# A hybrid decoder step on one Trainium2 core: the experts' weight units through six SBUF buffers instead of twelve

## The reference, cut to what matters

```python
def swiglu(x, wg, wu, wd):
    return (jax.nn.silu(x @ wg) * (x @ wu)) @ wd

def moe_swiglu(h, w_r, b_r, wg, wu, wd):
    ...
    top_p, top_e = lax.top_k(probs, TOP_K)              # 2 of 8 experts per token
    ...
    def expert_block(args):
        xblk, e = args
        return swiglu(xblk, wg[e], wu[e], wd[e])
    yb = lax.map(expert_block, (xb, block_e)).reshape(n_slots, dm)
    contrib = yb[dest] * sp[:, None].astype(h.dtype)
    return jax.ops.segment_sum(contrib, stok, num_segments=n_tok)
```

## Time and profile before

| | |
|---|---|
| timed runs, median | 1714.72 us |
| the profiled execution, its own time | 1708.33 us |
| its span, first to last instruction | 1706.5 us |
| TensorE busy | 1607.8 us (94%) |
| VectorE / ScalarE / GpSimd busy | 763.8 / 378.2 / 122.9 us |
| the experts' matmuls, from the first to the last | 790.6 to 1667.9 us |
| DMA moved | 535.7 MB, mean 314 GB/s |

### The profile page before, as it was taken

The page is one execution under the profiler, slowest core; times in us unless marked ns, Lnnn a source line. Parts: engine busy times, 40 slices in busy tenths (PEclk is TensorE's granted clock), DMA queues, the critical chain, the costliest instruction groups (busy, mean ns, idle before and its releaser), DMA issues.

```text
span 1706.5 us, 31161 instructions
## 1 busy us (share of the span) xinstructions
PE 1607.8 (94%) x12948; PEld 902.9 (53%) x12948; DVE 763.8 (45%) x1822; ACT 378.2 (22%) x616; POOL 122.9 (7%) x162
## 2 busy tenths in 40 slices
PE   6996299999999999999999999999999999999993
PEld 3874297899998879864333333333333333333331
DVE  2796155555443998362233422433234233342233
ACT  3444052544424453421001000010010100101012
POOL 0123210100002113011000000000000000000000
PEclk8998599999999999997999999999999999999997
DMA  9889812744455782054899999999999999999995
GB/s 383 348 314 338 290 41 101 300 158 162 173 198 213 282 324 115 7 220 177 325 407 391 420 420 412 420 410 421 420 405 420 412 415 420 407 419 415 413 421 221
DMA packets 82486, 535.73 MB, mean 314 GB/s; under 512 B 9200, under 2 KB 9328, under 8 KB 23600
## 3 DMA queue, kind: packets, MB, share of 16 engines
q1 hardware_dynamic: 70592, 487.46, 71.1%
q0 software_dynamic: 10080, 40.47, 6.5%
q10 hardware_dynamic: 1680, 5.90, 1.0%
HBM read 516.24 MB, written 36.43 MB: 324 GB/s over the span
## 4 chain that ended last, share of the span: by engine, by line
PE 79%; DVE 6%; ACT 1%; DMA 1%; issue 1%; POOL 0%; DVEq 0%; POOLq 0%
PE ps L2386 42%; PE ps L2395 5%; PE ps L2410 4%; PE ps L1871 4%; PE ps L1873 4%; PE ps L1872 4%; PE ps L2060 3%; DVE yc L1315 2%; PE ps L1968 1%; PE ps L1983 1%; PE ps L1981 1%; PE ps L2231 1%; PE ps L2001 1%; PE ps L2368 1%; DVE wlo L1222 1%
## 5 line engine op out<-in xcount | busy, mean ns | idle before, releaser
L2410 PE MATMUL ps<-raw,hT 128*32 128x512 f32 x1008 | 437.2, 592 | 0.0
L2410 PE MATMUL ps<-extra,hT 128*32 128x512 f32 x972 | 421.5, 592 | 0.0
L2386 PE MATMUL ps<-extra,ht 128*32 128x512 f32 x2736 | 403.2, 595 | 0.7 <-DVE ht L1797 0.7
L2386 PE MATMUL ps<-raw,ht 128*32 128x512 f32 x2640 | 387.1, 592 | 0.0
L1809 DVE TENSOR_TENSOR ae<-ps,sge 96x512 f32<-96x512 f32 x56 | 38.5, 687 | 536.7 <-PE ps L2386 536.7
L2386 PEld LDWEIGHTS ps<-extra,ht 128*32 128x32 f32 x2736 | 108.3, 110 | 270.2 <-issue 270.2
L2386 PEld LDWEIGHTS ps<-raw,ht 128*32 128x32 f32 x2640 | 104.1, 110 | 257.8 <-issue 257.8
L1792 DVE STREAM_TRANSPOSE hT<-ae 32x128 f32<-32x128 f32 x672 | 202.8, 302 | 15.7
L1191 ACT ACTIVATE sge<-ps 96x512 f32<-96x512 f32 x56 | 33.2, 593 | 706.9 <-PE ps L2386 706.7
L1871 PE MATMUL ps<-h_hi,whi 128*128 128x288 f32 x560 | 168.2, 300 | 0.2 <-DVE h_lo L1299 0.2
L1872 PE MATMUL ps<-h_lo,whi 128*128 128x288 f32 x560 | 165.9, 296 | 0.0
(11 more groups left out here) (346 smaller groups left out, 1774.4 us busy)
## 6 DMA issues: line engine op xcount, KB each, us to landing
raw<-units SPq DMA_DIRECT2D x279, 1024.0 KB, 11.4
extra<-units SPq DMA_DIRECT2D x174, 1024.0 KB, 13.2
slots_in<-const_in POOLq DMA_DIRECT2D x18, 512.0 KB, 26.3
slots_out<-const_in POOLq DMA_DIRECT2D x18, 512.0 KB, 27.6
raw<-units SPq DMA_DIRECT2D x16, 512.0 KB, 10.9
sst<-gdn_in POOLq DMA_DIRECT2D x8, 512.0 KB, 10.8
gdns_out<-sst POOLq DMA_DIRECT2D x8, 512.0 KB, 4.0
qst_out<-qpad POOLq DMA_DIRECT2D x2, 1890.0 KB, 10.7
```

Of the source, the lines that this page charges most:

```text
L2386: last = mm(ps[rows(t), (0 if kind == "g" else 2) + n % 2, :], ht[n // FC % 2][:, a], weights((kind, n, k // 4), k % 4), start=(k == 0), s ...
L2410: last = mm(ps[GROUPS * GT:P, DOWN_BANK[t][half], :], hidden(n, t, k), weights(("d", n, half), k), start=(c == 0 and first), stop=(n in (F ...
```

## The change

The ring has six buffers, `raw0` to `raw5`. The buffers `extra` and their semaphores are gone, and so is the loading of units in the middle of layer 1. In the loop a load waits for the unit six places ahead of it in `STREAM` instead of twelve. The matmuls, their order and the order of the units stay as they are. At the end six loads more than needed are issued instead of twelve.

```diff
-RING = 2 * NRAW
+RING = NRAW
...
-        extra = [at(f"extra{i}", cursor[0] + i * UNIT * 4, UNIT) for i in range(2 * NSPLIT)]
...
-        extra_in = [sem(f"extra_in{i}") for i in range(2 * NSPLIT)]
...
         def buffer_of(q):
 
-            i = q % RING
-            if i < 2 * NSPLIT:
-                return extra[i], extra_in[i], 16 * (q // RING + 1)
-            r = (U_MOE + i) % NRAW
+            r = (U_MOE + q) % NRAW
             return raw[r], raw_in[r], 16 * (len(range(r, U_MOE, NRAW)) + q // RING + 1)
...
-            split_end = SPLIT_UNITS[-1] + NRAW + 1
             for u in range(U_MOE):
                 load(u)
...
-                if u == split_end:
-                    sp.wait_ge(unit_used, S_MOE)
-                    for q in range(2 * NSPLIT):
-                        load_expert(q)
-            for q in range(2 * NSPLIT, RING):
-                wait_free(U_MOE - NRAW + q - 2 * NSPLIT)
+            for q in range(RING):
+                wait_free(U_MOE - NRAW + q)
                 load_expert(q)
...
-            wait_last(sp, range(2 * NSPLIT))
             sp.wait_ge(y_ready, 1)
             sp.dma_start(y_out[:, 0:KD * T // 2], hf[:, 0:KD * T // 2]).then_inc(y_sent, 16)
-            wait_last(sp, range(2 * NSPLIT + 1, RING))
+            wait_last(sp, range(1, RING))
...
-            _, landed_, value = buffer_of(2 * NSPLIT)
+            _, landed_, value = buffer_of(0)
             pool.wait_ge(landed_, pool.snap(n_pass * PER_BUFFER + value))
```

## The result

The changed kernel takes 1935.63 us (1932.68 and 1938.58), the one before 1714.72 us: a ratio of 1.130, interval 1.125 to 1.135. The forecast was 1846 us and its range ended at 1880. The direction was right, the size was not: 221 us instead of 131.

A forecast was written before the change was run, and what follows sets the result against it. TensorE was taken to set the pace, with the DMA engines nearly full. Stalls 132.3, experts' rows 4 and end -2 made 134 us on 1708.3, so 1842.6; forecast 1846 us, halfway to the timed median's offset, range 1824 to 1880.

The forecast's parts named there:

- What bounds the kernel: Experts' part: TensorE and DMA engines both nearly full; TensorE sets the pace, SyncE's loads wait for buffers still in use.
- The load's lead: Experts' part, slot 8: u0 lands late, TensorE stalls 2.45 us in each of 54 steps, 132.3 us in all.
- The fit of the Trainium skill: Weight loads: 2.0 us fixed plus bytes over 436 GB/s per DMA; stall 1.9 us, 103 us in sum; trace preferred.
- The granted clock: Rival, experts' part: clock falls to half in each stall, 127 us more, 1973 us; chance 0.12.
- The experts' rows: ScalarE's transfers once per expert push u1 0 to 0.9 us late in 7 steps; 4 us taken; what follows fits.
- The end: Kernel's end: fewer unneeded loads ahead of expert 7's last results; between 0 and -4.6 us, -2 taken.
- Slower batches: Rival, experts' part: DMA engines fall to 361 GB/s in short batches, stall 3.3 us, 1892 us; chance 0.07.
- no stall: Rival, experts' part: landing times are all backlog, u0 lands by T + 4.91, 1704 to 1714 us; chance 0.03.
- What would show it right or wrong: Signs in the experts' part: right, some 54 waits of about 2.3 us, clock 1.00; wrong, clock under 1.00, among others.
- the first rival: Experts' part: the granted clock falls in each stall, 127 us more, 1973 us; chance 0.12.
- the first case: Experts' part: one stall of 2.1 to 2.9 us per step, 113 to 157 us; chance 0.78.

The follow-up runs named there:

- lead6: The kernel before with all twelve buffers; only the loop's load waits for the unit six places ahead instead of twelve: 1938.82 us, ratio 1.132.
- fill2: The changed kernel plus two extra matmuls of constants between slot 7 and the wait of slot 8 in steps 2 to 55: 1898.96 us, ratio 1.110.
- rows16: On fill2, 16 instead of 96 rows of `xe` fetched from expert 2 on and of `ye` stored for experts 0 to 6: 1877.46 us.
- after_again: The changed kernel itself, run once more with nothing altered: 1939.24 us, ratio 1.134.
- ring7: The kernel before with a ring of seven buffers, the six raw ones and one extra, instead of twelve: 1803.88 us, ratio 1.052.

## Why the prediction was wrong, point by point

- **What bounds the kernel.** Right: both engines were nearly full, and the load's lead became the limit. lead6 shows it alone.
- **The load's lead, 54 x 2.45 = 132 us.** Right in mechanism, place and size. d0 landed 4.8 and u0 6.8 us after their issues, the step with nothing else in it is 17.95 us (17.90 predicted), and a typical stall is 2.2 us idle plus 0.17 us of restart: 54 x 2.37 = 128 us. The fit of the Trainium skill, page "DMA: Bandwidth & Descriptors", section on the anatomy of one DMA, is given there for DMAs that GpSimd issues, while these loads come from SyncE, which the prediction did not say. Its 4.4 us for one unit would have put the stall at 1.9 us; the trace did not agree.
- **The granted clock.** This is the step that failed: the sum and the range put it at nothing. I gave the fall a chance of 0.12, as a rival, because the clock was still full late in the idle stretch from 156 on the earlier trace rows. The two stretches of 2.2 and 2.5 us that were followed by the lower level were the nearer rows in length, and I set them aside for the sparse matmuls around them. In the changed kernel 16 of the 30 idle stretches of 1.95 to 2.3 us are followed by a fall, 9 of the 13 of 2.3 to 3 us and all 13 longer ones. Nor was it "always or never": the rival priced a fall in every step, 4.7 us long, at 127 us. In fact 38 stretches of 60 had one, 35 of them 3.4 us long and three 6.8, and the trace loses 67 us, of which fill2 got 37 back. A clock that is full during the idle stretch, as in the row from 156 on, also proves little, since most falls come only after the restart. With the clock kept up the time is still 1899 us, above the range's 1880, so the clock is the largest missing term and not the only one. The Trainium skill, "TensorE: Matmul & The Clock Gate", section "Why this matters for your kernels", warned of idle gaps between bursts of matmuls, because the clock can go back to half; the trace agrees, with 38 falls behind 60 stretches that lie between dense matmuls.
- **The experts' rows, 4 us.** The size came out by luck: the waits that follow them make 6.1 us in the changed kernel, but before g0 at slot 0, where I had said that all fits, and not before u1. With the clock kept up, five sixths of the rows cost 21.5 us (rows16).
- **Instruction fetches, not in the sum at all.** 10 stalls with a q8 packet are 1.4 us longer than the typical 2.2 and the seven with a q14 packet about 0.6 us: some 18 us. This is not shown as a cause: it rests on which stalls have a packet in their window, after_again and ring7 bear it out less, and no run took the fetches away.
- **The end, -2 us.** Right in size, by luck: 36.7 us from the last expert matmul to the end of the span, where it was 38.7. The gathering of the rows takes 4.61 us instead of 7.36; the last results still take 7.05, where I had expected the gain.
- **Slower batches, and no stall.** Neither rival came: 2.5 us a unit held in the short batches of the changed kernel, and the landing of a load was not all backlog.
- **What would show it right or wrong** named the clock under 1.00 as the sign of the first rival, and that is what came. The range ended at the first case's dearest value, and so left out the one case for which the trace had two rows.

## What to carry to other kernels

When a ring of buffers is made shorter, count for each load the time from its release to its first use, and set it against the time that one, two and three loads take to an empty queue; the number of buffers alone says little (the order of loading was worth 77 us at the same six). A regular wait of some two microseconds on TensorE can have a second price in the granted clock: look in the trace for idle stretches of that length and at the clock behind them too, and give their fall the weight that those rows have. And when two losses overlap, removing one yields less than its own sum, so measure it before promising it.

## What the runs showed of the hardware that was not expected

- TensorE with 1.7 us more work per step is faster by 37 us, because it does not stand still for as long (fill2).
- The same idle length, 2.0 to 2.3 us, is followed by a fall of the clock in one step and not in the next (16 of 30).
- In the changed kernel's first trace a 16 KB packet of instructions among the loads goes with a unit that lands 1.4 us later, where the unit alone takes 2.5 us of the queue; in ring7 it goes with 0.2 us.
- With the 384 KB transfers of ScalarE's queue among the weight units, the DMA engines move 359 GB/s at a share of 0.99, not 416.
